# HGRN stage of a hybrid decoder step: outer products by groups of 32 partitions, read-outs in halves

## The chip, the cores and the metric

The kernel runs on one core of one Trainium2 chip. The metric is the device time of one execution in microseconds; the time before is the median of three runs.

## What is computed

The reference is one inference step of a two-layer decoder trunk for 256 prompt tokens and 8 samples of 4 tokens, width 1024. Each layer has an adaLN-modulated norm, one input projection that feeds three parallel mixers (HGRN2, RG-LRU, gated DeltaNet), an output projection, and a retrieval of experts. The change touches the HGRN2 mixer alone, and the modulation product that is woven into it:

```python
mod = jax.nn.silu(c) @ p['w_ada'] + p['b_ada']          # six sections of 1024 columns, per layer
def hgrn2_chunked(q, k, v, log_f, S0):                  # 4 heads, key and value width 64
    def step(S, inp):
        qc, kc, vc, lf = inp
        G = jnp.cumsum(lf, axis=2); Gl = G[:, :, -1]
        o_inter = jnp.einsum('bhik,bhkv->bhiv', qc * jnp.exp(G), S)
        diff = G[:, :, :, None, :] - G[:, :, None, :, :]
        decay = jnp.exp(jnp.where(mask, diff, -jnp.inf))
        A = jnp.einsum('bhik,bhjk,bhijk->bhij', qc, kc, decay)
        o = o_inter + jnp.einsum('bhij,bhjv->bhiv', A, vc)
        S = S * jnp.exp(Gl)[..., None] + jnp.einsum('bhjk,bhjv->bhkv', kc * jnp.exp(Gl[:, :, None, :] - G), vc)
        return S, o
```

The kernel does this in blocks of 8 prompt tokens in place of the reference's chunks of 64: 32 blocks for the prompt, one of 4 tokens for each sample.

## The kernel before

Everything is float32. The program is a loop over the two layers, and each layer is a row of blocks with a barrier of all engines between them: projection, local mixer, `hgrn_block`, `delta_block`, output, experts, gates, combine. Inside a block each engine runs a list that is written out by hand, and semaphores tie the lists.

`hgrn_block` has four heads in two pairs; a pair fills 128 partitions (64 rows of head r = 0 and 64 of r = 1). C = 8 is the length of a block, BLOCKS = 32, TB = 16 blocks fill one tile of 128 tokens, HALF = 8. Its parts:

- **Distances** (line 1217). For d = 0 to 7 VectorE multiplies queries by keys d tokens earlier (`pairs`, L1324), TensorE sums over a head's 64 rows with a matrix of ones (`distance(d)`, 128x128), and VectorE multiplies by the values and adds (`values`, L1341 and L1344).
- **Outer products** (`products(step)`, L1262, four steps). A token tile `ktt` (128 tokens on partitions, 64 key columns of a head) is multiplied by `vm`: the values copied 8 times side by side, each copy masked to the 8 tokens of one block (`mask_v`, ScalarE, L1183; 8 copies for each of four steps, and 8 for the samples). One matmul is 128 rows by 64 columns with 512 moving columns, and gives the outer products of 8 blocks for one head. A step has four of them (two pairs, two heads) and fills two of the four PSUM banks of `ps_outer`. `sample_products` (L1272) does the same for the samples from 32 partitions.
- **The chain of states** (L1367). VectorE forms state b = decay times state b-1 + outer product b, 64 instructions of 128x64 for the 32 blocks and two pairs. Each counts up `after0` or `after1`.
- **Read-outs** (L1233). `read_states(turn)`: for each of 8 blocks and each head TensorE multiplies the 64x64 state by 8 columns of queries, 32 small matmuls; `read_samples` does it for the states of the samples, 4 columns each.
- **Modulation tiles** (`ada(first, end)`, L532). Tiles 8 to 31 of the modulation product, each four matmuls of 128x32 with 256 moving columns. Even tiles come from `ring` (3 slots), odd ones from `extra_ring` (4 slots); the SyncE queue loads a slot again when its tile is done. After each eight tiles ScalarE copies the rows out (L556), TensorE turns them (`turn(n)`, L542), ScalarE copies the columns (L563), and the next tile after that waits for `cols_out`.

The order of TensorE decides the order of the rest. The four vm-turns use two buffers, and `mask_v` of the third turn waits for the products of the first. At the end VectorE waits for `inter_ready`, which the last read-out counts up, and adds the read-outs to the output (L1379).

`keep_busy(pe, m, out, n)` issues n bf16 matmuls of 512 columns that nobody reads. It is called in other blocks before the change.

In the rows below a float32 matmul stands as two records: the four matmuls of a products step are x8, and the 32 of a read-out are x64.

Of the kernel before, what the change touches and what calls it, by code (L numbers as in the profile page):

```python
# [27 lines left out]
P = 128  # L28
# [9 lines left out]
HD = 64  # L38
# [172 lines left out]
@contextmanager  # L211
def signals(nc, m, names):

    ctx = ExitStack()
    m.stage += 1
    sems = {n: ctx.enter_context(nc.semaphore(f"{n}_of_{m.stage}")) for n in names.split()}
    clear_retired(nc, m)
    yield sems
    m.retired.append((ctx, sems))
# [332 lines left out]
def copy_rows(act, m, s, rows, ps, n):  # L552

    e = (KD * n + KD - 1) // 2
    act.wait_ge(m.xdone[e % XRING], e // XRING + 1)
    act.activation(rows, ps[:, 0:2 * P], ACT.Copy).then_inc(s["rows_out"], 1)  # L556


def copy_columns(act, m, s, ps, n, done):

    act.wait_ge(s["cols_ready"], done)
    dst, src = ada_columns(m, SECTIONS[n], ps)
    act.activation(dst, src, ACT.Copy).then_inc(s["cols_out"], 1)  # L563
# [403 lines left out]
def keep_busy(pe, m, out, n):  # L967

    operand = m.keep[:, 0:2 * P].bitcast(BF16)
    for _ in range(n):  # L970
        pe.matmul(out, operand[:, 0:P], operand, start=True, stop=True)
# [145 lines left out]
def hgrn_block(nc, m, l, extra, stream, ps_mod):  # L1117
# [5 lines left out]
    names = ("step sums_ready turned kt_out values_done vm_ready u_ready after0 after1 samples_u sample_free sample_read "  # L1123
             "kept0 kept1 inter_ready products_ready rows_out cols_ready cols_out")
    HALF = TB // 2
    with signals(nc, m, names) as s, nc.psum_tensor("ps_sums", [P, 3, 512], F32) as ps_sums, \
            nc.psum_tensor("ps_outer", [P, 4, 512], F32) as ps_outer, nc.Block() as block:
        gate, key, since, qt, kt = m.hgate, m.hkey, m.since, m.qt, m.kt
        q = m.zact[:, 0:2, :]
        f = Area(m.big, m.after_local)  # L1130
        after = f.take(A_PAIRS, BLOCKS, HD)
        vm = f.take(2, 4, TB // 2, HD)
        pair_p = f.take(2, 2 * NP)
        pair_s = f.take(2, 2 * NB * NS)
        prod_p = f.take(2 * NP)
# [29 lines left out]
        @block.scalar  # L1165
        def _(act):
            for tt in range(3):
                n = TOK[tt][1]
                act.wait_ge(s["turned"], tt + 1)
                act.activation(flat(ktt[0:n, tt, :, :]), ps_outer[0:n, tt, 0:2 * P], ACT.Copy)  # L1170
                act.activation(vtok[0:n, tt, :], ps_outer[0:n, tt, 2 * P:4 * P], ACT.Copy).then_inc(s["kt_out"], 1)

            def mask_v(turn):

                if turn < 4:
                    tt, first, n, mask = turn // 2, turn % 2 * TB // 2, P, m.mix("block_rows")
                else:
                    tt, first, n, mask = 2, 0, NB * NS, m.mix("batch_rows")
                if turn >= 2:
                    act.wait_ge(s["u_ready"], 2 * turn - 2)  # L1180
                values = vtok[0:n, tt, :].rearrange("p (h v) -> p h v", h=4)
                for b in range(TB // 2):
                    i = act.activation(vm[0:n, turn % 2, :, b, :], values, ACT.Copy, scale=mask[0:n, first + b:first + b + 1])  # L1183
                i.then_inc(s["vm_ready"], 1)

            act.wait_ge(s["kt_out"], 3)
            mask_v(0)
            copy_rows(act, m, s, ada_rows, ps_mod, 1)
            copy_columns(act, m, s, ps_mod, 1, 1)
            mask_v(1)  # L1190
            mask_v(2)
            mask_v(3)
            copy_rows(act, m, s, ada_rows, ps_mod, 2)
            copy_columns(act, m, s, ps_mod, 2, 2)
            mask_v(4)
            copy_rows(act, m, s, ada_rows, ps_mod, 3)
            copy_columns(act, m, s, ps_mod, 3, 3)
            for pair in range(A_PAIRS):
                act.wait_ge(s[f"after{pair}"], BLOCKS)
            act.activation(m.states[:, 0:A_PAIRS, 0, :], after[:, :, BLOCKS - 1, :], ACT.Copy)  # L1200

        @block.gpsimd
        def _(pool):
# [6 lines left out]
        def _(pe):  # L1210
# [9 lines left out]
            def ada(first, end):  # L1220
                for i in range(first, end):
                    if i % KD == 0 and i > LOCAL_ADA:
                        pe.wait_ge(s["cols_out"], (i - LOCAL_ADA) // KD)
                    ada_tile(pe, m, extra, i, ps_mod)
# [7 lines left out]
                rows = slice(r * HD, (r + 1) * HD)  # L1232
                return pe.matmul(out[rows], state[rows], qt[rows, pair, t:t + n], start=True, stop=True)  # L1233

            def read_samples():

                pe.wait_ge(s["sample_free"], 1)
                for b in range(NB):
                    for pair in range(A_PAIRS):
                        for r in range(2):  # L1240
                            mm = inter(sample_inter(pair)[:, NS * b:NS * (b + 1)], pair, r, NP + NS * b, NS,
                                       m.state0[:, pair, b, :])
                mm.then_inc(s["sample_read"], 1)

            def read_states(turn):

                for pair in range(A_PAIRS):
                    pe.wait_ge(s[f"after{pair}"], HALF * (turn + 1))
                for b in range(turn * HALF + 1, min((turn + 1) * HALF + 1, BLOCKS)):
                    for pair in range(A_PAIRS):  # L1250
                        for r in range(2):
                            mm = inter(ps_sums[:, pair, C * b:C * (b + 1)], pair, r, C * b, C, after[:, pair, b - 1, :])
                return mm

            def products(step):
                pe.wait_ge(s["vm_ready"], step + 1)
                for pair in range(A_PAIRS):
                    if step >= 2:
                        pe.wait_ge(s[f"after{pair}"], HALF * (step - 1))
                    for r in range(2):  # L1260
                        rows = slice(r * HD, (r + 1) * HD)
                        mm = pe.matmul(ps_outer[rows, (2 * step + pair) % 4, :], ktt[:, step // 2, pair, rows],  # L1262
                                       vm[:, step % 2, 2 * pair + r, :, :], start=True, stop=True)
                    mm.then_inc(s["u_ready"], 1)

            def sample_products():
                pe.wait_ge(s["vm_ready"], 5)
                for pair in range(A_PAIRS):
                    pe.wait_ge(s[f"after{pair}"], HALF * 3)
                    for r in range(2):  # L1270
                        rows = slice(r * HD, (r + 1) * HD)
                        mm = pe.matmul(ps_outer[rows, pair, :], ktt[0:NB * NS, 2, pair, rows],  # L1272
                                       vm[0:NB * NS, 0, 2 * pair + r, :, :], start=True, stop=True)
                    mm.then_inc(s["samples_u"], 1)

            for tt, (t0, n) in enumerate(TOK):
                for pair in range(A_PAIRS):
# [8 lines left out]
            distance(2)  # L1286
            ada(11, 12)
            distance(3)
            ada(12, 14)
            distance(4)  # L1290
            ada(14, 16)
            distance(5)
            products(0)
            distance(6)
            turn(1)
            distance(7)
            read_samples()
            ada(16, 20)
            products(1)
            ada(20, 24)  # L1300
            products(2)
            turn(2)
            pe.wait_ge(s["values_done"], 1)
            read_states(0)
            ada(24, 27)
            products(3)
            read_states(1)
            ada(27, 29)
            sample_products()
            ada(29, 32)  # L1310
            read_states(2)
            turn(3)
            mm = read_states(3)
            mm.then_inc(s["inter_ready"], 1)

        @block.vector
        def _(ve):
# [36 lines left out]
            values(C - 1)  # L1354
            steps.wait(steps.n)
            ve.sem_inc(s["values_done"], 1)
            for turn in range(4):
                ve.wait_ge(s["u_ready"], 2 * turn + 2)
                for b in range(turn * HALF, (turn + 1) * HALF):
                    for pair in range(A_PAIRS):  # L1360
                        new, j = after[:, pair, b, :], b % HALF
                        add = ps_outer[:, (2 * turn + pair) % 4, j * HD:(j + 1) * HD]
                        if b == 0:
                            i = ve.tensor_copy(new, add)
                        else:
                            ve.wait_ge(s[f"after{pair}"], b)
                            i = ve.scalar_tensor_tensor(new, after[:, pair, b - 1, :],  # L1367
                                                        since[:, pair, C * b + C - 1:C * b + C], add, ALU.mult, ALU.add)
                        i.then_inc(s[f"after{pair}"], 1)
# [1545 lines left out]
def host_layout(a):  # L2915
# [65 lines left out]
    def const(name, value):  # L2981
        v = np.asarray(value, f)
        mixc[:v.shape[0], MIXC[name][0]:MIXC[name][1]] = v
# [19 lines left out]
    const("neg_s", np.where(same, 0.0, -1e30))  # L3003
    const("eye_c", jc == ic)
    const("eye_s", js == i_s)
    const("block_rows", j // 8 == np.arange(P // 8)[None, :])
    tok = np.arange(NB * NS) // NS
    const("batch_rows", np.tile(tok, 2)[:, None] == np.arange(NB)[None, :])
    heads_of = np.zeros((P, 6, 12))
# [65 lines left out]
```

## Time and profile before

| | us |
|---|---|
| median of three runs | 2321.52 (2315.86 to 2324.93) |
| profiled execution, its time | 2320.4 |
| profiled execution, its span | 2318.2 |
| HGRN block, layer 0, in that span | 151.57 to 194.40 |
| HGRN block, layer 1, from the first distance | 1293.90 to 1337.12 |

The span is the time from the first to the last instruction in the profile; the execution's own time has 2.2 us more around it. All times in the text are in microseconds from the span's start. PE is TensorE's matmuls, PEld its weight loads, DVE VectorE, ACT ScalarE.

### The profile page before, as it was taken

How to read it: one execution, taken by the hardware profiler on the slowest of the kernel's cores; microseconds unless marked ns; L12 is line 12 of the kernel's file. 1: busy time of each engine (PE TensorE's matmuls, PEld its weight loads, DVE VectorE, ACT ScalarE, POOL GpSimd, SP SyncE). 2: the span in 40 equal slices, each digit the busy share in tenths (PEclk: the TensorE clock that was granted, in tenths of full speed). 3: DMA queues.
4: the chain of work that ended last, by engine and by line, in shares of the span. 5: the costliest groups of instructions: out<-in, count | busy, mean ns of one | idle time of the engine just before them, and what ended most of it. 6: DMA issues, size and time to landing. Idle time of an engine off the chain costs nothing. (4 is left out here: it accounts for less than half of the span.)

```text
span 2318.2 us, 58007 instructions
## 1 busy us (share of the span) xinstructions
PE 2247.4 (97%) x20562; PEld 2076.7 (90%) x20562; DVE 1495.5 (65%) x3062; ACT 1267.3 (55%) x2437; POOL 1088.8 (47%) x990
## 2 busy tenths in 40 slices
PE   7999999999999999999989999999999999999998
PEld 4967779999998899999978586899999988999997
DVE  3876339943227878788668663598322296887885
ACT  3652225576558855555556422455855596555554
POOL 0221018864446656566304010498444474665661
PEclk8999999999999999999999889999999999999999
DMA  7472135555553389899454702455555534998982
GB/s 290 155 254 94 65 132 182 180 199 185 187 189 137 109 275 312 274 310 314 163 181 160 277 5 102 155 182 181 199 189 185 189 109 139 310 312 272 308 300 100
DMA packets 123816, 455.53 MB, mean 197 GB/s; under 512 B 13745, under 2 KB 14257, under 8 KB 122545
## 3 DMA queue, kind: packets, MB, share of 16 engines
q1 hardware_dynamic: 105264, 386.80, 46.9%
q0 software_dynamic: 18432, 67.12, 10.6%
q8 instruction: 79, 1.29, 0.2%
q14 instruction: 41, 0.33, 0.0%
HBM read 449.37 MB, written 4.49 MB: 196 GB/s over the span
## 5 line engine op out<-in xcount | busy, mean ns | idle before, releaser
L446 POOL TENSOR_TENSOR parts<-ring,parts 128x512 fp32r<-128x512 f32 x358 | 463.4, 1298 | 469.5 <-ACT parts L439 455.7
L439 ACT ACTIVATE parts<-ring 128x512 fp32r<-128x512 f32 x620 | 389.3, 632 | 352.3 <-PE ps_u L493 281.2
L489 PE MATMUL ps_u<-h_parts,parts 128*128 128x256 f32 x4096 | 563.1, 280 | 0.9 <-ACT parts L439 0.6
L2739 PE MATMUL ps_y<-act_parts,parts 128*128 128x256 f32 x4096 | 563.6, 280 | 0.0
L489 PEld LDWEIGHTS ps_u<-h_parts,parts 128*128 128x128 f32 x4096 | 514.7, 188 | 3.2 <-ACT parts L439 1.9
L2739 PEld LDWEIGHTS ps_y<-act_parts,parts 128*128 128x128 f32 x4096 | 515.8, 188 | 0.8 <-ACT parts L2679 0.7
L446 DVE TENSOR_TENSOR parts<-ring,parts 128x512 fp32r<-128x512 f32 x262 | 187.1, 720 | 360.5 <-ACT parts L439 336.1
L2788 POOL TENSOR_TENSOR act_parts<-big,act_parts 128x256 fp32r<-128x256 f32 x256 | 245.0, 957 | 306.2 <-ACT act_parts L2768 306.2
L493 PE MATMUL ps_u<-h_parts,parts 128*128 128x256 f32 x2048 | 322.2, 279 | 1.2 <-DVE parts L446 0.9
L2743 PE MATMUL ps_y<-act_parts,parts 128*128 128x256 f32 x2048 | 322.5, 279 | 0.0
L493 PEld LDWEIGHTS ps_u<-h_parts,parts 128*128 128x128 f32 x2048 | 275.5, 188 | 2.0 <-DVE parts L446 1.3
L2743 PEld LDWEIGHTS ps_y<-act_parts,parts 128*128 128x128 f32 x2048 | 276.3, 188 | 0.0
L2686 DVE TENSOR_TENSOR parts<-ring,parts 128x512 fp32r<-128x512 f32 x260 | 213.4, 843 | 75.1 <-ACT parts L2679 74.4
L2686 DVE TENSOR_TENSOR parts<-more_ring,parts 128x512 fp32r<-128x512 f32 x252 | 208.7, 848 | 74.7 <-ACT parts L2679 74.7
L2768 ACT ACTIVATE act_parts<-big 128x256 fp32r (+1 forms) x256 | 107.1, 418 | 221.3 <-PE ps_y L2743 216.2
L2679 ACT ACTIVATE parts<-ring 128x512 fp32r<-128x512 f32 x260 | 162.0, 624 | 50.2 <-PE ps_y L2743 50.2
L2679 ACT ACTIVATE parts<-more_ring 128x512 fp32r<-128x512 f32 x252 | 157.4, 625 | 46.0 <-PE ps_y L2743 46.0
L2574 POOL TENSOR_TENSOR onehot<-keep,sel 128x512 f32<-128x512 f32 x128 | 132.8, 1040 | 49.1 <-PE ps_g L2546 36.1
L2546 PEld LDWEIGHTS ps_g<-onehot 128*128 128x128 f32 x1024 | 134.5, 195 | 17.0 <-issue 13.5
L2546 PE MATMUL ps_g<-onehot 128*128 128x128 f32 x1024 | 139.7, 280 | 4.8 <-ACT onehot L2587 4.1
L489 PE MATMUL ps_z<-x_parts,parts 128*128 128x288 f32 x864 | 132.9, 296 | 1.4 <-ACT parts L439 1.4
L489 PEld LDWEIGHTS ps_z<-x_parts,parts 128*128 128x128 f32 x864 | 121.0, 188 | 2.0 <-ACT parts L439 1.7
(410 smaller groups left out, 2824.5 us busy)
## 6 DMA issues: line engine op xcount, KB each, us to landing
ring<-in_stream SPq DMA_DIRECT2D x506, 512.0 KB, 3.4
more_ring<-in_stream SPq DMA_DIRECT2D x126, 512.0 KB, 3.5
extra_ring<-in_stream SPq DMA_DIRECT2D x32, 512.0 KB, 5.9
mod_ring<-in_stream SPq DMA_DIRECT2D x32, 512.0 KB, 3.3
big<-in_stream SPq DMA_DIRECT2D x16, 512.0 KB, 11.5
out_state_out<-big SPq DMA_DIRECT2D x2, 1440.0 KB, 8.1
big<-in_state SPq DMA_DIRECT2D x2, 1280.0 KB, 10.8
big<-in_mixc SPq DMA_DIRECT2D x2, 1024.0 KB, 8.3
```

Of the source, the lines that this page charges most:

```text
L439: eng.activation(m.parts[:, q % PARTS, 0, :], half_tile(m, t, half), ACT.Copy).then_inc(s["hi_ready"], 1)
L446: eng.tensor_tensor(m.parts[:, q % PARTS, 1, :], half_tile(m, t, half), m.parts[:, q % PARTS, 0, :].bitcast(F32), ALU.subtract).then_inc(m ...
L489: pe.matmul(out, hi[:, k, :], hr[:, side, kk, 0:tokens], start=(kk + side == 0), stop=False)
L493: mm = pe.matmul(out, lo[:, k, :], hr[:, 0, kk, 0:tokens], start=False, stop=(kk == KD - 1))
L2546: mm = pe.matmul(ps_g[:, q % SETS, c, :], first[:, q % SETS, c, :], second[:, q % SETS, c, :], start=True, stop=True)
L2574: pool.tensor_tensor(second[:, g % SETS, :, :], spread(m.iota, 1, GROUP), spread(tokens_of(m.second_key, i, g), 2, P), ALU.subtract).then_ ...
L2679: act.activation(m.parts[:, q % PARTS, 0, :], tile[:, half * D // 2:(half + 1) * D // 2], ACT.Copy).then_inc(s["hi_ready"], 1)
L2686: v.tensor_tensor(m.parts[:, q % PARTS, 1, :], tile[:, half * D // 2:(half + 1) * D // 2], m.parts[:, q % PARTS, 0, :].bitcast(F32), ALU.s ...
L2739: pe.matmul(ps[:, half * KD // 2 + k, :], hi[:, k, :], act_parts[:, j % AHEAD, side, :], start=False, stop=False)
L2743: mm = pe.matmul(ps[:, half * KD // 2 + k, :], lo[:, k, :], act_parts[:, j % AHEAD, 0, :], start=False, stop=False)
L2768: act.activation(act_parts[:, j % AHEAD, 0, :], column(g, j), ACT.Copy).then_inc(s["act_hi"], 1)
L2788: pool.tensor_tensor(act_parts[:, j % AHEAD, 1, :], column(g, j), act_parts[:, j % AHEAD, 0, :].bitcast(F32), ALU.subtract).then_inc(s["ac ...
```

## The change

The mask is now by groups of 32 partitions: `block_rows` is periodic, so four masked copies serve all four groups of a token tile, and both token tiles get their copies at once (8 copies in place of 32; the samples have a buffer of their own). An outer-product matmul has 32 rows (the tokens of 4 blocks), 64 columns and 256 moving columns; the four row groups write to the four banks. There are three calls with 16, 8 and 8 matmuls in place of four with 4. `sample_products` is issued pair by pair in two places. The read-outs come in halves (4 blocks each, the samples' too) and stand between short runs of modulation tiles; the first half of the samples' stands between distances 3 and 4. `turn(3)` goes behind the last read-out, with four matmuls of `keep_busy` after it.

```diff
-            def mask_v(turn):
-                if turn < 4:
-                    tt, first, n, mask = turn // 2, turn % 2 * TB // 2, P, m.mix("block_rows")
-                else:
-                    tt, first, n, mask = 2, 0, NB * NS, m.mix("batch_rows")
-                if turn >= 2:
-                    act.wait_ge(s["u_ready"], 2 * turn - 2)
-                for b in range(TB // 2):
-                    i = act.activation(vm[0:n, turn % 2, :, b, :], values, ACT.Copy, scale=mask[0:n, first + b:first + b + 1])
+            def mask_v(tt):
+                for j in range(GROUP):
+                    i = act.activation(vm[:, tt, :, j, :], values, ACT.Copy, scale=m.mix("block_rows")[:, j:j + 1])
+            def mask_samples():
+                for b in range(NB):
+                    i = act.activation(vms[0:n, :, b, :], values, ACT.Copy, scale=m.mix("batch_rows")[0:n, b:b + 1])
             act.wait_ge(s["kt_out"], 3)
             mask_v(0)
+            mask_v(1)
             copy_rows(act, m, s, ada_rows, ps_mod, 1)
             copy_columns(act, m, s, ps_mod, 1, 1)
-            mask_v(1)
-            mask_v(2)
-            mask_v(3)
+            mask_samples()
...
-            def read_states(turn):
+            def read_states(turn, half):
+                first = turn * HALF + half * GROUP + 1
                 for pair in range(A_PAIRS):
-                    pe.wait_ge(s[f"after{pair}"], HALF * (turn + 1))
-                for b in range(turn * HALF + 1, min((turn + 1) * HALF + 1, BLOCKS)):
+                    pe.wait_ge(s[f"after{pair}"], first + GROUP - 1)
+                for b in range(first, min(first + GROUP, BLOCKS)):
...
-            def products(step):
-                pe.wait_ge(s["vm_ready"], step + 1)
+            def products(tt, first, end):
+                pe.wait_ge(s["vm_ready"], tt + 1)
                 for pair in range(A_PAIRS):
-                    if step >= 2:
-                        pe.wait_ge(s[f"after{pair}"], HALF * (step - 1))
-                    for r in range(2):
-                        rows = slice(r * HD, (r + 1) * HD)
-                        mm = pe.matmul(ps_outer[rows, (2 * step + pair) % 4, :], ktt[:, step // 2, pair, rows],
-                                       vm[:, step % 2, 2 * pair + r, :, :], start=True, stop=True)
-                    mm.then_inc(s["u_ready"], 1)
+                    if tt:
+                        pe.wait_ge(s[f"after{pair}"], GROUP * end)
+                for pair in range(A_PAIRS):
+                    for group in range(first, end):
+                        tokens = slice(32 * group, 32 * group + 32)
+                        for r in range(2):
+                            rows = slice(r * HD, (r + 1) * HD)
+                            mm = pe.matmul(ps_outer[rows, group, pair * GROUP * HD:(pair + 1) * GROUP * HD],
+                                           ktt[tokens, tt, pair, rows], vm[tokens, tt, 2 * pair + r, :, :], start=True, stop=True)
+                mm.then_inc(s["u_ready"], 1)
+            def sample_products(pair):
+                pe.wait_ge(s["vm_ready"], 3)
+                for other in range(A_PAIRS):
+                    pe.wait_ge(s[f"after{other}"], TB + GROUP * (pair + 1))
...
             distance(3)
-            ada(12, 14)
+            pe.wait_ge(s["sample_free"], 1)
+            read_samples(0, NB // 2)
             distance(4)
+            ada(12, 13)
+            distance(5)
+            products(0, 0, 4)
+            distance(6)
+            ada(13, 14)
+            distance(7)
             ada(14, 16)
-            distance(5)
-            products(0)
-            distance(6)
+            read_samples(NB // 2, NB).then_inc(s["sample_read"], 1)
             turn(1)
-            distance(7)
-            read_samples()
-            ada(16, 20)
-            products(1)
-            ada(20, 24)
-            products(2)
+            ada(16, 17)
+            pe.wait_ge(s["values_done"], 1)
+            read_states(0, 0)
+            ada(17, 19)
+            products(1, 0, 2)
+            read_states(0, 1)
+            ada(19, 21)
+            read_states(1, 0)
+            ada(21, 22)
+            products(1, 2, 4)
+            ada(22, 24)
+            read_states(1, 1)
             turn(2)
-            pe.wait_ge(s["values_done"], 1)
-            read_states(0)
+            sample_products(0)
             ada(24, 27)
-            products(3)
-            read_states(1)
+            read_states(2, 0)
             ada(27, 29)
-            sample_products()
-            ada(29, 32)
-            read_states(2)
+            read_states(2, 1)
+            ada(29, 30)
+            sample_products(1)
+            ada(30, 32)
+            read_states(3, 0)
+            read_states(3, 1).then_inc(s["inter_ready"], 1)
             turn(3)
-            mm = read_states(3)
-            mm.then_inc(s["inter_ready"], 1)
+            keep_busy(pe, m, ps_outer[:, 3, :], 4)
...
-            for turn in range(4):
-                ve.wait_ge(s["u_ready"], 2 * turn + 2)
-                for b in range(turn * HALF, (turn + 1) * HALF):
+            for first, ready in ((0, 1), (TB, 2), (TB + HALF, 3)):
+                ve.wait_ge(s["u_ready"], ready)
+                for b in range(first, TB if ready == 1 else first + HALF):
...
-    const("block_rows", j // 8 == np.arange(P // 8)[None, :])
+    const("block_rows", j // 8 % 4 == np.arange(P // 8)[None, :] % 4)
```

On ScalarE the copy of the last state now stands ahead of the third `copy_rows`, in place of behind it.

## Rows read from the trace of the kernel before

**Rows 1.** The page: busy time, share and instructions of each engine.

```profile
PE 2247.4 (97%) x20562; PEld 2076.7 (90%) x20562; DVE 1495.5 (65%) x3062; ACT 1267.3 (55%) x2437; POOL 1088.8 (47%) x990
```

**Rows 2.** Windows: HGRN block of layer 0, then the delta block's start in both layers.

```profile
core 0: us, PE busy (x) PEld busy (x) DVE busy (x) ACT busy (x) POOL busy (x), PEclk, DMA share, GB/s
151.57:194.40 42.83, 39.81 (x592) 23.64 (x593) 27.26 (x103) 19.71 (x54) 2.50 (x2) 1.00 0.76 282
194.40:203.06 8.66, 8.64 (x128) 5.84 (x128) 5.20 (x12) 2.31 (x3) 0.00 (x0) 0.61 0.01 2
...
1337.12:1344.52 7.40, 7.38 (x128) 5.19 (x128) 5.20 (x12) 2.32 (x3) 0.00 (x0) 0.72 0.01 2
```

**Rows 3.** Timeline, TensorE, layer 0 (start, length, engine, line, what, records).

```profile
139.69 5.13 PE L971 MATMUL ps_q<-keep 128*128 128x512 bf16 x23
...
168.57 0.64 PE L532 MATMUL ps_mod<-ring,cond 128*32 128x256 f32 x8
...
170.43 1.94 PE L1262 MATMUL ps_outer<-big 128*64 128x512 f32 x8
...
172.30 0.64 PE L532 MATMUL ps_mod<-ring,cond 128*32 128x256 f32 x8
...
174.17 1.94 PE L1262 MATMUL ps_outer<-big 128*64 128x512 f32 x8
...
176.59 0.64 PE L542 MATMUL ps_mod<-keep,big 128*128 128x36 f32 x4 [0.48 <-ACT big L556]
...
188.68 2.04 PE L1233 MATMUL ps_sums<-big 64*64 64x8 f32 x64
190.65 0.64 PE L542 MATMUL ps_mod<-keep,big 128*128 128x36 f32 x4
191.21 1.80 PE L1233 MATMUL ps_sums<-big 64*64 64x8 f32 x56
194.42 0.99 PE L1486 MATMUL ps_delta<-big 128*128 128x6 f32 x4 [1.41 <-PEq L1127]
```

**Rows 4.** Timeline, VectorE, layer 0.

```profile
167.12 0.28 DVE L1344 TENSOR_TENSOR big<-big 128x64 f32<-128x64 f32 x1
...
172.42 3.16 DVE L1367 SCALAR_TENSOR_TENSOR big<-big,ps_outer 128x64 f32<-128x64 f32 x16 [1.84 <-PE ps_outer L1262]
...
193.06 0.67 DVE L1379 TENSOR_TENSOR big<-big,ps_sums 128x496 f32<-128x496 f32 x1 [4.94 <-PE ps_sums L1233]
```

**Rows 5.** Windows, TensorE alone: two stretches of 64x64 matmuls in the delta block.

```profile
core 0: us, PE busy (x), PEclk, DMA share, GB/s
201.36:202.95 1.59, 1.59 (x97) 1.00 0.03 10
206.08:207.63 1.55, 1.55 (x51) 1.00 0.04 11
```

**Rows 6.** Timeline, ScalarE, layer 0: masked copies, and columns after a turn.

```profile
154.01 3.31 ACT L1183 ACTIVATE big<-big 128x256 f32<-128x256 f32 x8
...
177.26 0.24 ACT L563 ACTIVATE mod<-ps_mod 128x72 f32<-128x72 f32 x1 [0.72 <-PE ps_mod L542]
```

**Rows 7.** DMA issues from 160 to 194 (KB each, median us to landing).

```profile
ring<-in_stream SPq DMA_DIRECT2D x10, 512.0 KB, 3.5
```

**Rows 8.** Windows around falls of the granted clock (columns as in rows 2).

```profile
190.97:194.39 3.42, 2.04 (x59) 1.91 (x59) 0.67 (x1) 0.44 (x3) 0.00 (x0) 1.00 0.05 16
194.39:197.80 3.41, 3.38 (x18) 2.57 (x18) 2.95 (x7) 1.27 (x1) 0.00 (x0) 0.50 0.00 0
...
1310.54:1313.96 3.42, 3.42 (x24) 1.18 (x18) 1.14 (x6) 3.42 (x10) 0.00 (x0) 0.50 0.73 247
```

**Rows 9.** Timeline, TensorE, layer 1.

```profile
1309.67 0.64 PE L532 MATMUL ps_mod<-ring,cond 128*32 128x256 f32 x8
...
1315.04 0.64 PE L532 MATMUL ps_mod<-ring,cond 128*32 128x256 f32 x8
...
1333.40 2.34 PE L1233 MATMUL ps_sums<-big 64*64 64x8 f32 x56
```

More of the change, by code:

```diff
@@ L1125, in hgrn_block @@
     HALF = TB // 2
+    GROUP = 32 // C
     with signals(nc, m, names) as s, nc.psum_tensor("ps_sums", [P, 3, 512], F32) as ps_sums, \
@@ L1131, in hgrn_block @@
         after = f.take(A_PAIRS, BLOCKS, HD)
-        vm = f.take(2, 4, TB // 2, HD)
+        vm = f.take(2, 4, GROUP, HD)
+        vms = f.take(4, NB, HD)
         pair_p = f.take(2, 2 * NP)
@@ L1171, in _ @@
                 act.activation(vtok[0:n, tt, :], ps_outer[0:n, tt, 2 * P:4 * P], ACT.Copy).then_inc(s["kt_out"], 1)
-            def mask_v(turn):
-                if turn < 4:
-                    tt, first, n, mask = turn // 2, turn % 2 * TB // 2, P, m.mix("block_rows")
-                else:
-                    tt, first, n, mask = 2, 0, NB * NS, m.mix("batch_rows")
-                if turn >= 2:
-                    act.wait_ge(s["u_ready"], 2 * turn - 2)
-                values = vtok[0:n, tt, :].rearrange("p (h v) -> p h v", h=4)
-                for b in range(TB // 2):
-                    i = act.activation(vm[0:n, turn % 2, :, b, :], values, ACT.Copy, scale=mask[0:n, first + b:first + b + 1])
+            def mask_v(tt):
+                values = vtok[:, tt, :].rearrange("p (h v) -> p h v", h=4)
+                for j in range(GROUP):
+                    i = act.activation(vm[:, tt, :, j, :], values, ACT.Copy, scale=m.mix("block_rows")[:, j:j + 1])
+                i.then_inc(s["vm_ready"], 1)
+            def mask_samples():
+                n = NB * NS
+                values = vtok[0:n, 2, :].rearrange("p (h v) -> p h v", h=4)
+                for b in range(NB):
+                    i = act.activation(vms[0:n, :, b, :], values, ACT.Copy, scale=m.mix("batch_rows")[0:n, b:b + 1])
                 i.then_inc(s["vm_ready"], 1)
@@ L1187, in _ @@
             mask_v(0)
+            mask_v(1)
             copy_rows(act, m, s, ada_rows, ps_mod, 1)
             copy_columns(act, m, s, ps_mod, 1, 1)
-            mask_v(1)
-            mask_v(2)
-            mask_v(3)
+            mask_samples()
             copy_rows(act, m, s, ada_rows, ps_mod, 2)
             copy_columns(act, m, s, ps_mod, 2, 2)
-            mask_v(4)
-            copy_rows(act, m, s, ada_rows, ps_mod, 3)
-            copy_columns(act, m, s, ps_mod, 3, 3)
             for pair in range(A_PAIRS):
@@ L1200, in _ @@
             act.activation(m.states[:, 0:A_PAIRS, 0, :], after[:, :, BLOCKS - 1, :], ACT.Copy)
+            copy_rows(act, m, s, ada_rows, ps_mod, 3)
+            copy_columns(act, m, s, ps_mod, 3, 3)
         @block.gpsimd
@@ L1233, in inter, with read_samples @@
                 return pe.matmul(out[rows], state[rows], qt[rows, pair, t:t + n], start=True, stop=True)
-            def read_samples():
-                pe.wait_ge(s["sample_free"], 1)
-                for b in range(NB):
+            def read_samples(first, end):
+                for b in range(first, end):
                     for pair in range(A_PAIRS):
@@ L1242, in read_samples @@
                                        m.state0[:, pair, b, :])
-                mm.then_inc(s["sample_read"], 1)
-            def read_states(turn):
+                return mm
+            def read_states(turn, half):
+                first = turn * HALF + half * GROUP + 1
                 for pair in range(A_PAIRS):
-                    pe.wait_ge(s[f"after{pair}"], HALF * (turn + 1))
-                for b in range(turn * HALF + 1, min((turn + 1) * HALF + 1, BLOCKS)):
+                    pe.wait_ge(s[f"after{pair}"], first + GROUP - 1)
+                for b in range(first, min(first + GROUP, BLOCKS)):
                     for pair in range(A_PAIRS):
@@ L1266, in sample_products @@
-            def sample_products():
-                pe.wait_ge(s["vm_ready"], 5)
-                for pair in range(A_PAIRS):
[L1269 to L1274, printed above, removed]
+                    if tt:
+                        pe.wait_ge(s[f"after{pair}"], GROUP * end)
@@ new lines, in products @@
+                mm.then_inc(s["u_ready"], 1)
[3 more added lines that the diff above has]
+                    pe.wait_ge(s[f"after{other}"], TB + GROUP * (pair + 1))
+                for r in range(2):
+                    rows = slice(r * HD, (r + 1) * HD)
+                    mm = pe.matmul(ps_outer[rows, pair, :], ktt[0:NB * NS, 2, pair, rows],
+                                   vms[0:NB * NS, 2 * pair + r, :, :], start=True, stop=True)
+                mm.then_inc(s["samples_u"], 1)
@@ L1356, in _ @@
             ve.sem_inc(s["values_done"], 1)
-            for turn in range(4):
-                ve.wait_ge(s["u_ready"], 2 * turn + 2)
-                for b in range(turn * HALF, (turn + 1) * HALF):
+            for first, ready in ((0, 1), (TB, 2), (TB + HALF, 3)):
+                ve.wait_ge(s["u_ready"], ready)
+                for b in range(first, TB if ready == 1 else first + HALF):
                     for pair in range(A_PAIRS):
-                        new, j = after[:, pair, b, :], b % HALF
-                        add = ps_outer[:, (2 * turn + pair) % 4, j * HD:(j + 1) * HD]
+                        new = after[:, pair, b, :]
+                        add = ps_outer[:, b // GROUP % 4, (pair * GROUP + b % GROUP) * HD:(pair * GROUP + b % GROUP + 1) * HD]
                         if b == 0:
```

## The prediction

> **What bounds the kernel now.** I read the page first: TensorE is busy 97% of the span, VectorE 65%, ScalarE 55% [rows 1]. The reader is to see that only what shortens TensorE's list, or lets it run at full clock, can shorten the kernel. Then the window of the block that is changed, in layer 0: of its 42.83 us TensorE is busy 39.81, VectorE 27.26 and ScalarE 19.71 [rows 2]. Then the timeline of TensorE, in which I take the time of a piece from its start to the next piece's start, since the lengths overlap [rows 3]. Last VectorE's timeline: it waits 1.84 us for outer products in one place and 4.94 us for the last read-outs [rows 4], so the block ends by TensorE's list, then one VectorE instruction (193.06 to 193.73), then the barrier: TensorE starts the next block at 194.42, 0.69 later.
>
> **Pieces of TensorE's list** [rows 3]. Four modulation tiles: 168.57 to 170.43, 1.86. An outer-product step: 170.43 to 172.30, 1.87. A read-out of 8 blocks: 188.68 to 190.65, 1.97. A turn: 190.65 to 191.21, 0.56. Each contains a fixed part. A bf16 matmul of 512 columns takes 0.216 (23 of them 5.13, the last one 0.38 of it), one cycle of 2.4 GHz a column. A step's eight float32 records of 512 columns, the two heads' side by side, take 1.87 / 4 = 0.47 a pair of records, so two cycles a column, 0.427, and a rest: 4 x 0.427 = 1.71 and 0.16, which goes into the change of piece; for four modulation tiles it is 1.86 - 4 x 0.427 = 0.15. I take 0.15 for every change between shapes of tiles.
>
> **Outer products.** Before, four steps stream 4 x 1.71 = 6.83 a layer. After, 32 matmuls of 256 columns do it. One tile of 32 rows by 64 columns then has, in each of the three calls, two matmuls of two records of 256 columns: 4 x 0.213 = 0.85. If the tiles run side by side the three calls stream 3 x 0.85 = 2.56, which saves 4.27. If matmuls that share columns and differ in rows run one after the other, the 32 are 16 head pairs of 0.427, 6.83 again, and nothing is saved. The trace has no 32-row tiles of this kind, but it has 64-row ones: in the first stretch of [rows 5] all four 64x64 tiles are in use, and 97 records take 1.59 us, 16 ns each; in the second only the two diagonal ones, and 51 take 1.55 us, 30 ns each. Same matmul, twice the rate when the rows differ too. With eight tiles a record of the new call is due each 0.85/32 = 27 ns, slower than the 16 ns already reached, so issue is no bound. I take the full 4.27; the bounds are 0 and 4.27.
>
> The Trainium skill says as much (TensorE: Matmul & The Clock Gate, Part 3, packing small matmuls), and gives 3.07x for four row tiles; by that factor the first call would stream 0.85 x 4 / 3.07 = 1.11, 0.26 us a layer more, an estimate from that page. No row here shows that factor. The Trainium skill also speaks against the change (TensorEngine Tiling, Key Properties): a change of tiling mode drains the engine. By the trace that is within the 0.15 us above.
>
> **More changes of piece.** From distance 0 to the end I count 29 pieces before and 40 after: 5 more runs of modulation tiles, 4 more read-outs, 2 more of 128x128 (distance 6, the turn and distance 7 were one). 11 x 0.15 = 1.65; the read-outs' fixed part is rather 0.11 (1.97 less 64 records at 29 ns), so 1.5. The bounds are 0 (if the loads ahead hide them) and 2.2 (11 x 0.20, what a full 128-column load would add).
>
> **Waits.** Before, step 3 ends at about 174.17 + 1.87 = 176.04 and turn(2) starts at 176.59, 0.55 late, since it waits for the copy of rows; after, a read-out lies between, and this goes. But turn(1) now stands right ahead of tile 16, which waits for ScalarE's columns: the copy starts 0.67 after the turn and takes 0.24 [rows 3, 6], so tile 16 starts 0.99 after turn(1) where 0.56 would do: +0.43. Turn(3) goes behind the last read-out, so VectorE's last addition comes 0.56 sooner.
>
> Sum to VectorE's last addition: -4.27 + 1.5 - 0.55 + 0.43 - 0.56 = **-3.45**: it starts at about 189.6 and ends at 190.3.
>
> **What else must keep up.** The VectorE chain: 16 instructions in 3.16 [rows 4], so 0.395 a block, 12.6 for 32. In my list of starts the last distance is at 165.3, its values end near 166.4 (167.40 before), and half the chain ends at 172.8. The second call needs blocks 0 to 7 (169.7) and runs at 171.3 to 172.3; the third runs at 176.0 to 177.0, where VectorE waits about 1.1; the chain ends at 180.3, and the last read-outs, which need it, are due at 187.7. It has 7 us to spare. The masked copies: 8 take 3.31 [rows 6]; 24 fewer spare ScalarE 9.9 us that nobody waited for, and both sets are there at 157.3, six us before use. The loads: the ring slot of tile 24 is free at 181.1 and its next load, tile 30, is used at 186.9, against 3.5 from issue to landing [rows 7]; other tiles have more. With a wait there it would cost up to 1 us.
>
> **The end of the block.** Behind the last read-out (189.4) come turn(3), 0.56, and four busy matmuls. At 0.216 each these are 0.86: TensorE ends at about 190.9, 0.6 behind VectorE. If the barrier takes the same 0.69, the next block starts at 191.6, **2.8 sooner** than 194.42. The two layers have the same list: **-5.6**.
>
> **The clock.** In 190.97 to 194.39 TensorE streams almost nothing (read-outs of 8 columns, then 1.41 idle), and from 194.39 it has half clock, 1.2 GHz [rows 3, 8]. The delta block's first pieces take 8.66 in layer 0 at a mean clock of 0.61, that is 6.8 us at the half level, and 7.40 at 0.72, 4.1 us, in layer 1 [rows 2]. So each us at the half level costs (8.66 - 7.40) / (6.8 - 4.1) = 0.47 us: 3.2 in layer 0, 1.9 in layer 1. Layer 1's last read-out is longer too, 2.34 for 1.80 [rows 3, 9]: 0.5. A further fall is in the middle of layer 1's block, 1310.54 to 1313.96 [rows 8], behind the uncut read-out of the samples; tiles 16 to 19 and one outer step take 5.37 there (1309.67 to 1315.04) and 3.73 in layer 0 (168.57 to 172.30) [rows 3, 9]: 1.6. Together 7.3 us. The change cuts the read-outs in two between denser pieces, and the end has 0.86 us of full columns and some 0.7 idle in place of 1.41. Yet read-outs and a turn still fill 2.3 us there, so I count on two thirds of the 7.3: **-4.9**. The bounds are 0 and -7.3, plus up to 2 more falls elsewhere, of 1.6 each.
>
> Sum: 2320.4 - 5.6 - 4.9 = 2309.9 for the profiled execution. The median of the runs is 1.1 above it, so I predict **2311**.
>
> **Rivals.**
> - The order helps and the clock doesn't: it falls at the ends as before. For it: the sparse 2.3 us. Then 2321.5 - 5.6 = 2316 (2313 to 2319). Chance 0.25.
> - All clock is kept, in the delta block too, which has sparse stretches that depend on where it starts: 2321.5 - 5.6 - 7.3 - 2 = 2306 or less. Chance 0.12.
> - Slower: row groups don't run side by side. Then 4.27 a layer isn't saved, and from -2.8 becomes +1.5: +3.0 in two layers, 2324.5 with no clock regained. It decides from the point at which the three calls save less than 2.8 a layer. Against it speak [rows 5]. Chance 0.05.
> - VectorE becomes the bound. If the third call came so late that the chain's last 3.16 us stood ahead of the last read-outs, each us over the 7 of slack would be lost. Its price would be all of the gain, 2319 to 2322; chance 0.04. The Trainium skill (TensorEngine Tiling, PSUM Bottleneck) says that tiling speeds TensorE and not the emptying of its banks; by [rows 4] the slack is there.
> - New falls of the clock in the middle, two of 1.6 a layer, and none regained: 2321.5 - 5.6 + 6.4 = 2322. Chance 0.04.
>
> The forecast's own case, 2307 to 2315, has 0.50.
>
> **How the numbers follow.** 0.5% of 2321.5 is 11.6 us, about what a measurement of this kernel can tell from no change (the three runs lie 9 us apart). Faster than that is below 2309.9: the 0.12 of the case with all clock kept and about half of the forecast's 0.50, in all 0.36. Slower than that, above 2333, needs the slower rival and more: 0.02. The rest, 0.62, is within. The range 2304 to 2320 leaves out the best part of the second case and the slow ones.
>
> **What would show it.** L1262 as 32 rows by 64 columns: 32 records in about 1.1 us for the first call, against 8 in 1.94; were it 3.4, the row groups were serial. VectorE's last addition at about 189.6 in layer 0. The next block 2.8 sooner. Granted clock 1.00 in the stretch after it. If the clock there is 0.5 in both layers, the time is 2316; if the block is shortened by less than 2, the changes of piece cost more than 0.15 each.

## The result, and the profile after

The changed kernel takes 2339.96 us (median of 9 runs, 2330.20 to 2343.52) against 2319.05 (9 runs): ratio 1.0084, 95% interval 1.0072 to 1.0095. It is **slower** by 21 us, 0.8%, where 2311 was forecast and 2304 to 2320 was the range. The profiled execution has a span of 2338.1.

Windows of the changed kernel: layer 0's block from the first distance, split at 171.2, and layer 1's from the fall of the clock on (columns as in [rows 2]):

```profile
155.67:171.20 15.53, 15.20 (x214) 9.14 (x214) 13.12 (x50) 4.83 (x14) 0.00 (x0) 1.00 0.76 246
171.22:215.60 44.38, 44.08 (x439) 25.49 (x437) 14.94 (x61) 5.28 (x13) 0.00 (x0) 0.50 0.47 158
...
1321.51:1365.90 44.39, 44.09 (x442) 25.52 (x439) 15.02 (x61) 5.38 (x13) 0.00 (x0) 0.50 0.49 164
```

The reader is to see the granted clock: 1.00 for 15.5 us, then 0.50 for 44.4, and the same again in layer 1. Before, the whole block of layer 0 ran at 1.00 [rows 2].

Timeline, TensorE, of the changed kernel, layer 0:

```profile
164.74 1.12 PE L1268 MATMUL ps_outer<-big 32*64 32x256 f32 x32
...
168.14 1.10 PE L1235 MATMUL ps_sums<-big 64*64 64x4 f32 x32
169.17 0.64 PE L542 MATMUL ps_mod<-keep,big 128*128 128x36 f32 x4
170.13 0.64 PE L532 MATMUL ps_mod<-ring,cond 128*32 128x256 f32 x8 [0.33 <-ACT mod L563]
170.70 1.48 PE L1235 MATMUL ps_sums<-big 64*64 64x8 f32 x32
172.11 1.08 PE L532 MATMUL ps_mod<-extra_ring,cond 128*32 128x256 f32 x8
172.97 1.08 PE L532 MATMUL ps_mod<-ring,cond 128*32 128x256 f32 x8
173.98 1.98 PE L1268 MATMUL ps_outer<-big 32*64 32x256 f32 x16
...
210.01 0.99 PE L1504 MATMUL ps_delta<-big 128*128 128x6 f32 x4 [0.30 <-PEq L1128]
```

The first call of outer products, 32 records of 32 rows by 64 columns, takes 1.12 us. It does the work of two of the four steps of before, 1.94 each [rows 3]. Up to here everything is as worked out. Then come, one behind the other, a read-out, a turn, a wait of 0.33 for the columns, one tile and a read-out. From 171.2 on, at half clock, each piece takes nearly twice its time, and none of the runs of modulation tiles that follow is longer than three.

### The profile page after: what moved, and what is told of

The parts are those of the page before. It is cut to its first block and busy times, and to the rows that moved or that the text cites. A ratio compares the mean times of both kernels' runs of the same rounds, so it can differ in the third digit from the quotient of the medians.

```text
span 2338.1 us, 58111 instructions
## 1 busy us (share of the span) xinstructions
PE 2269.9 (97%) x20634; PEld 2087.2 (89%) x20634; DVE 1496.9 (64%) x3062; ACT 1248.2 (53%) x2389; POOL 1092.3 (47%) x990
```

## The experiments

Theories A and B are stated in the first expectation, C and D in the fifth. The kernel before was timed again with each group of runs, and each ratio is to those times. Each run has one profiled execution.

`fill(n)` issues n bf16 matmuls of 192 columns that nobody reads ("busy matmuls"), 80 to 90 ns each, and some 0.1 us more for the change of piece. Where it is used, VectorE adds the samples' read-outs behind `inter_ready` (not in the third run).

**1. The order alone.**

```diff
-products(0, 0, 4); products(1, 0, 2); products(1, 2, 4)
+products(0); products(1) ... products(2) ... products(3)      # 128 rows, 512 columns, in these places
```

> The new order of TensorE's list and the halved read-outs, but the outer products by 128 rows as before (a third buffer for the masked values, so that no step waits for a buffer). Theory A (the order holds the clock down: short runs of modulation tiles between read-outs never make a dense stretch, so the clock doesn't come back after its fall at turn(1)): half clock for 20 us or more in each layer's block, some 2340 to 2350 us. Theory B (the row-group products do it, because they take 4.3 us of full columns out of a layer): the clock stays, only the pieces cost, 2318 to 2324 us.

2326.44 us (2308.01 to 2336.69), ratio 1.0026 (1.0001 to 1.0051). Both theories are off: the order costs a third of the loss, and the executions lie far apart. Of its 7 us the prediction's sum gives 3 to the pieces (the -5.6 without the 8.5 that the row groups save). In its profile the clock falls at 174.7 and is back after 3.4 us, in which TensorE did a tile and one outer-product step of 128 rows (175.54, 3.22 us); it falls again at 188.4 and stays at half for 23.9 us. Layer 1 shows the same: 3.3 us from 1318.2, with a step, and 23.9 from 1331.7.

**2. The row groups alone.**

```diff
-products(0) ... ada(16, 20); products(1); ada(20, 24); products(2) ... products(3)
+products(0, 0, 4) ... ada(16, 24); products(1, 0, 2) ... products(1, 2, 4)     # the rest in the old order
```

> The products by 32 rows in the order of before: whole read-outs, tiles 16 to 23 in one run, turn(3) ahead of the last read-out, no busy matmuls. Theory A: the clock falls as it did before, at the ends and perhaps once in the middle, so the 4.3 us a layer stay as a gain: 2308 to 2314 us. Theory B: half clock through the block, above 2330 us.

2335.23 us (2319.33 to 2340.02), 1.0054 (1.0028 to 1.0080). Theory A, that the order does it, has fallen, since the old order loses as well. The time is what theory B expected, but this run's timeline, TensorE, shows a possible cause that neither theory had:

```profile
171.99 0.61 PE L532 MATMUL ps_mod<-extra_ring,cond 128*32 128x256 f32 x8
174.99 1.08 PE L532 MATMUL ps_mod<-ring,cond 128*32 128x256 f32 x8 [2.39 <-DMA ring<-in_stream]
```

With no outer products between them, tiles 16 to 23 come faster than the loads. TensorE idles 2.39 us, and has half clock from 175.0 to 216.0. In layer 1 it idles 2.80 us at the same place and the clock falls too, but it comes back for 3 us in the middle of the later call on two row groups, behind three tiles:

```profile
1335.19 1.25 PE L1268 MATMUL ps_outer<-big 32*64 32x256 f32 x16
```

Such a call takes 1.98 at half clock and 1.09 at full. The changed kernel has no such wait.

**3. Busy matmuls round turn(1).**

```diff
 read_samples(NB // 2, NB).then_inc(s["sample_read"], 1)
+fill(12)
 turn(1)
+fill(6)
```

> The changed kernel with 12 bf16 matmuls of 192 columns ahead of turn(1) and 6 behind it, some 1.4 us of added work in a layer, part of it in the 0.4 us wait for the columns. If the fall at turn(1) is what starts the 44 us of half clock and the rest of the order holds a full clock, the time drops to 2305 to 2318 us. If the order behind it loses the clock by itself, the fall only moves to a later place and the time stays at 2330 to 2345 us.

2320.62 us (2306.62 to 2328.14), 0.9997 (0.9976 to 1.0018): a little above what was expected, and 19 us less than the changed kernel, for 1 us a layer of work more. The clock now holds to 188.4, and falls there, in the stretch of the samples' products and halved read-outs, for 17 us. In layer 1 it holds to 1335.3, the last turn, and is at half for 10 us. The run also gives the changed order's starts at full clock (its timeline, TensorE):

```profile
155.54 1.29 PE L1219 MATMUL ps_sums<-big 128*128 128x512 f32 x4 [1.12 <-DVE big L1349]
...
178.29 1.09 PE L1268 MATMUL ps_outer<-big 32*64 32x256 f32 x16
```

The third call starts 22.75 behind the first distance. The prediction had it at 176.0, 21.77 behind its 154.23; the busy matmuls ahead of the turn add 1.0 (169.04 to 170.04).

**4. The tail alone**, in the kernel before.

```diff
-turn(3); read_states(3)
+read_states(3); turn(3); keep_busy(pe, m, ps_outer[:, 3, :], 4)
```

> The kernel before with only its tail changed: turn(3) behind the last read-out and four busy matmuls. VectorE's last addition 0.56 earlier, TensorE's end about 0.3 to 0.8 later. If the busy matmuls hold the clock at the block's end: 3 to 5 us less, 2314 to 2317 us. If not: 2318 to 2322 us.

2318.52 us, 0.9989 (0.9974 to 1.0003): nothing that can be told from none. In its profile the clock is at half from 195.1 to 205.3: the busy matmuls (196.41) come when it has already fallen, behind two whole read-outs in a row. An earlier fall, at 181.4, ended after 3.3 us, in a 128-row step (182.47, 3.10 us).

**5. Busy matmuls where the row groups took work out**, in the second run's kernel.

```diff
 products(0, 0, 4)
+fill(11)
-ada(16, 24)
+ada(16, 20); fill(21); ada(20, 24)
 products(1, 0, 2)        # and the same behind products(1, 2, 4)
+fill(11)
```

> The second run's kernel (products by 32 rows in the old order, 2335 us) with 54 busy bf16 matmuls of 192 columns a layer, some 4.3 us, in the places from which the row groups took the streaming of 128 rows; the samples' addition stands behind the last read-out, 0.5 us later. Theory C (what counts is how much of the time all 128 rows are fed; the row groups took 4.3 us of that out, so the clock falls and doesn't return): the clock is that of the kernel before, 0.98 to 0.99, and the time 2316 to 2324 us, less than without the added work. Theory D (the 32-row shape itself keeps the clock down): the clock stays at 0.973 to 0.981 and the time is 2340 us or more.

2317.48 us (2312.41 to 2323.71), 0.9999 (0.9987 to 1.0012): theory C. 4.7 us a layer of work that nobody reads (the four fills of its timeline, each to the next piece's start) gives back 18 us. It doesn't show by which way, since the busy matmuls also slow the tiles, and the wait for the load shrinks from 2.39 to 0.60 us.

**6. The second token tile in one call**, in the changed kernel.

```diff
-ada(17, 19); products(1, 0, 2); read_states(0, 1); ada(19, 21); read_states(1, 0); ada(21, 22); products(1, 2, 4); ada(22, 24)
+ada(17, 19); read_states(0, 1); ada(19, 21); products(1, 0, 4); read_states(1, 0); ada(21, 24)
```

> The changed kernel with the second token tile's products in one call of 16 matmuls over all four row groups, in place of two calls that use two row groups each. 0.85 us of streaming and one change of piece less a layer. Theory C: the call feeds 128 rows for 0.85 us where two calls fed 64 for 1.7, the sum is the same, and the read-outs round it are as sparse: the clock falls at turn(1) as in the changed kernel, 2330 to 2342 us. If the half-filled calls are what keeps the clock down: 2315 to 2325 us.

2317.56 us (2305.50 to 2324.93), 0.9994 (0.9975 to 1.0013). Theory C as I had put it, a sum of work, missed this: the first fall is where it was, but the clock comes back. Two windows of this run, of layer 0:

```profile
171.60:178.40 6.80, 6.80 (x94) 3.90 (x100) 2.45 (x13) 1.63 (x5) 0.00 (x0) 0.50 0.88 331
178.40:188.70 10.30, 9.87 (x214) 6.16 (x200) 7.02 (x35) 0.93 (x3) 0.00 (x0) 1.00 0.87 295
```

And its timeline, TensorE, where they meet, and at the same call and the return of the clock in layer 1:

```profile
177.29 1.63 PE L1268 MATMUL ps_outer<-big 32*64 32x256 f32 x32
178.85 1.10 PE L1235 MATMUL ps_sums<-big 64*64 64x8 f32 x32
...
1317.91 2.01 PE L1268 MATMUL ps_outer<-big 32*64 32x256 f32 x32
...
1324.38 1.50 PE L1235 MATMUL ps_sums<-big 64*64 64x8 f32 x32
```

In layer 0 the clock comes back in the middle of the one call that feeds all four row groups. The changed kernel's calls feed two groups, 64 of 128 rows, for the same sum, and the clock stayed down through both. But in layer 1 the clock falls at 1311.8, the joined call passes wholly at half clock, and full clock is back only at 1325.2, behind three tiles in a row, which this edit makes too (`ada(21, 24)` in place of one and two). So the run shows that the clock can come back in this order; it doesn't show that the joined call is what brings it back. In layer 0 it falls again at 188.7, for 17 us.

**7. Busy matmuls throughout**, in the changed kernel: `fill` of 2 to 12 at twelve places between its pieces (74 a layer; the 72 of the expectation is a miscount) and two more in `keep_busy` at the end. The samples' second read-out goes behind turn(1); all shapes are kept.

```diff
-read_samples(NB // 2, NB).then_inc(s["sample_read"], 1)
+fill(6)
 turn(1)
+fill(2)
+read_samples(NB // 2, NB).then_inc(s["sample_read"], 1)
 ada(16, 17)
+fill(4)
...
-keep_busy(pe, m, ps_outer[:, 3, :], 4)
+keep_busy(pe, m, ps_outer[:, 3, :], 6)
```

> The changed kernel with busy matmuls of 192 columns at twelve places, 72 a layer and two more at the end, some 8 us of added work a layer with the changes of piece. Theory C: no sparse stretch is left, the clock stays full in both blocks (0.99), and the time is 2319.5 - 5.6 - 7.3 + 17 = 2324 us or a little less: 16 us of work added and 16 us less time than the changed kernel. Otherwise 2345 us or more.

2318.81 us (2314.51 to 2322.56), 1.0002 (0.9991 to 1.0012). Some 7 us of work more a layer by its timeline, and 21 us less time than the changed kernel. Windows of this run, over both layers' blocks:

```profile
153.00:199.00 46.00, 45.06 (x707) 28.98 (x708) 26.32 (x105) 10.14 (x26) 0.45 (x1) 1.00 0.73 248
1296.00:1342.00 46.00, 45.64 (x795) 29.92 (x788) 26.70 (x105) 7.84 (x19) 0.00 (x0) 1.00 0.67 227
```

The granted clock is 1.00 in both. So the 32-row shape doesn't keep it down, nor does the order if its gaps are filled.

**8 to 10, 12. An order made for the clock**: one call for the second tile; the samples' second read-out behind turn(1), in the wait for the columns; sparse pieces apart. The whole list from tile 14 on:

```python
 ada(14, 16); fill(5); turn(1); read_samples(NB // 2, NB); ada(16, 19); read_states(0, 0); ada(19, 21); read_states(0, 1)
 products(1, 0, 4); ada(21, 22); read_states(1, 0); ada(22, 24); sample_products(0); turn(2); fill(5); ada(24, 26)
 read_states(1, 1); ada(26, 27); sample_products(1); ada(27, 29); read_states(2, 0); ada(29, 31); fill(4)
 read_states(2, 1); fill(10); read_states(3, 0); ada(31, 32); fill(6); read_states(3, 1); turn(3); keep_busy(..., 4)
 # 9: also fill(4) behind ada(21, 22), fill(5) ahead of ada(26, 27) and of ada(27, 29)
 # 10: none of the fills;  12: as 9, and fill(6) ahead of and behind ada(19, 21)
```

> An order made from theory C: the second tile's products in one call, no two sparse pieces side by side where a run of tiles can stand between them, and 30 busy matmuls of 192 columns a layer round the turns and the last read-outs. Work a layer at full clock: the changed kernel's 2.8 us gain, less 2.9 for the busy matmuls, their changes of piece and the samples' addition at the end, plus 1.0 for the single call. Theory C: the clock holds in most executions, 2308 to 2316 us. If it falls at turn(1) all the same: 2325 us or more.

> The even order with 14 more busy matmuls of 192 columns a layer (44 in all), at three places in the stretch in which the second layer's clock fell at 1316.1 in the even order's profile. Some 1.7 us a layer of work more with the changes of piece, partly in a wait for a load. Theory C: the fall goes, all executions lie at a clock of 0.988 or more, 2308 to 2314 us. If this has no effect on the clock: 2319 to 2322 us.

> The even order without any of the 30 busy matmuls (the four at the end stay): what the order alone does. Theory C: stretches with two sparse pieces come back round the turns and the last read-outs, the clock falls in more executions, 0.980 to 0.985, and the 2.9 us a layer of work that is saved is lost again: 2314 to 2322 us. If the order alone holds the clock: 2306 to 2311 us.

> The even order with 44 busy matmuls and 12 more a layer round tiles 19 and 20, where the first layer's clock fell at 173.6 in that run's profile; 0.96 us and some 0.4 for the changes of piece a layer. Theory C: that fall goes as well; all executions at 0.988 or more, 2309 to 2314 us, and none above 2320. If the few slow executions of the run before have another cause, they stay.

| busy matmuls a layer | median (range), us | ratio, 95% interval |
|---|---|---|
| 0 (run 10) | 2318.16 (2311.56 to 2333.36) | 1.0001 (0.9989 to 1.0012) |
| 30 (run 8) | 2317.73 (2304.61 to 2324.50) | 0.9987 (0.9966 to 1.0008) |
| 44 (run 9) | 2312.27 (2305.51 to 2331.51) | 0.9984 (0.9965 to 1.0004) |
| 56 (run 12) | 2312.98 (2307.91 to 2318.31) | **0.9977 (0.9965 to 0.9989)** |

Each step adds work, and none adds time that can be told from noise. Run 8 was above its range of 2308 to 2316. Run 9's median was in its range, but not all its executions. Run 12 has none above 2320, though two have a mean clock of 0.987, below the 0.988 expected; its profile's clock is 1.00 in layer 0's block up to 193.9 and in layer 1's up to 1330.5. It is the only version shown faster than both kernels, by 5 us of the kernel before and 27 of the changed one. It is the best of four tries, and runs 9 and 12 can't be told apart. Run 10 differs from the other three in VectorE's list too, which is that of the changed kernel.

Run 10's profiled execution, its slowest (2333.36), speaks against the joined call as the thing that ends a fall. Two windows of it:

```profile
172.80:210.20 37.40, 36.77 (x356) 20.90 (x348) 12.53 (x46) 3.24 (x7) 0.00 (x0) 0.50 0.44 157
1319.80:1357.20 37.40, 36.77 (x384) 21.82 (x382) 11.87 (x45) 2.71 (x6) 0.00 (x0) 0.50 0.44 159
```

The joined call stands right at the start of the first (172.62), and the clock stays at half for 37.4 us in each layer.

**11. One call, and turn(1) covered.**

```diff
-ada(14, 16); read_samples(NB // 2, NB); turn(1)      # in run 6's kernel
+ada(14, 16); fill(5); turn(1); read_samples(NB // 2, NB)
```

> The changed kernel with two changes: the second tile's products in one call, and five busy matmuls ahead of turn(1) with the samples' second read-out behind it, in the wait for the columns. The first alone gave 2317.6 us. Theory C: the fall at turn(1), 7 to 14 us of half clock a layer in that run's profile, goes: 2309 to 2315 us. Otherwise 2316 us or more.

2315.71 us (2311.39 to 2327.43), 1.0006 (0.9990 to 1.0021). The median is just above the 2309 to 2315 expected, and the ratio shows no gain over run 6. The clock falls at 170.6 all the same, so covering turn(1) alone doesn't prevent the early fall.

## Why the prediction was wrong

**Right: the pieces.** The row groups run side by side: 32 records in 1.12 us, 1.05 to the next piece, 1.01 worked out (0.85 streamed, 0.16 for the change). The estimate by the factor 3.07, 1.11 of streaming, isn't borne out: 1.05 less 0.16 leaves 0.89. The wait for the columns: tile 16 starts 0.96 behind turn(1), 0.99 worked out. The third call in run 3 is within 0.1 of its worked-out place. VectorE's chain has its 0.36 + 5.83 for the first 16 blocks, and TensorE never waited for the chain. Run 7 gives the whole block at full clock: 44.23 from the first distance (153.59) to the next block (197.82), of which 7.3 are its fills and 0.4 its two more matmuls in `keep_busy`; 36.5 are left, against 40.19 - 2.8 = 37.4 worked out. So -5.6 for two layers stands as the gain of the pieces at full clock, and the rival of serial row groups is out. One reading was wrong and small: "other tiles have more" time for their loads than tile 30, yet in run 3 tile 28 waits 0.45 for its load. A check: mean clocks of 0.984 before and 0.972 after are 2 x 0.016 x 2318 = 74 and 2 x 0.028 x 2338 = 131 us at the half level. 57 us more at the prediction's 0.47 is 27 us; the span grew by 19.9, so some 7 us of gain is hidden in it.

**Wrong: the step "I count on two thirds of the 7.3: -4.9", with the bounds "0 and -7.3, plus up to 2 more falls elsewhere, of 1.6 each".** The sign was wrong: with -5.6 from the pieces and a span 19.9 longer, the clock's term was about +25, not -4.9. Each fall was priced as one of 3.4 us, because in the kernel before the fall of 1310.54 ended by 1313.96 [rows 8]. I didn't ask what TensorE did while it lasted. Timeline of the kernel before:

```profile
1310.56 1.10 PE L532 MATMUL ps_mod<-ring,cond 128*32 128x256 f32 x8
...
1312.45 2.66 PE L1262 MATMUL ps_outer<-big 128*64 128x512 f32 x8
```

There it did the last two of four tiles in a row and then an outer-product step of 128 rows, in whose course the clock came back. The change takes such stretches away. In the changed kernel the fall at 171.2 met only runs of one to three tiles, calls on half the rows and read-outs, so 44.4 us passed, to the delta block's wide matmuls. From the first distance to the next block it is 54.34 (155.67 to 210.01) against 40.19 before, 14.2 more although the pieces save 2.8: a fall priced at 1.6 cost some 17 in layer 0's block. The rival "new falls of the clock in the middle" had the right place and the wrong price, and a chance of 0.04.

**What the change did to the clock.** Shown: the time went to the clock, and the loss begins at turn(1). Run 7 keeps the shapes and, but for one read-out, the order, has full clock through both blocks, and is 21 us faster than the changed kernel with more work. In the changed kernel half a read-out, the turn, 0.33 idle, one tile and half a read-out lie in a row there; run 3, which fills that place, has its falls 17 and 21 us later behind the first distance, is at half clock for 17 and 10 us in place of 44 and 44, and gets 19 us back.

Not shown: which part of the change keeps the clock down once it has fallen. The nearest reading is that steps of 128 rows became calls on 64. For it: in runs 1 and 4, and in the kernel before, a fall in the middle ended within 3.4 us, in such a step, and run 6, which joins two calls, gets 22 us back, some 2 of them for the work that it spares. Against it: in run 2's layer 1 the clock came back in a call on 64 rows; in run 6's layer 1 and all through run 10's profile the joined call didn't bring it back. The longer run of tiles in run 6 is a rival that no run tests apart. The order alone costs 7 us (run 1). That it does so by spreading halved read-outs between short runs of tiles is argued from its timeline, not shown. Run 7 shows that neither shape nor order matters where no sparse stretch is left.

**Left open:** how much of run 2's loss is its wait for a load, and why executions of one kernel differ so much (those of run 8 lie 20 us apart, those of run 9 26, with mean clocks from 0.981 to 0.991 and 0.980 to 0.992). Only one execution of each has a profile, so where the others lose the clock isn't known, and a fall seen in one profile, or missing from it, is one draw.

## What to carry to other kernels

Where TensorE bounds the kernel, packing its matmuls so that they take less time can also take away the dense stretches that kept its clock up; here a saving of 2.8 us a layer came with a loss of some 17 in layer 0. Price a fall of the clock by what follows it, and look in the trace for what TensorE did when the falls that are there ended: it was 3.4 us in one order and 44.4 in another. When sparse pieces must be issued, try them one at a time between long runs, and try some matmuls that nobody reads: here 56 of them, 5.7 us a layer by run 12's timeline, gained 5 us by the medians over the same order without them.

## What the runs showed of the hardware

- Eight tiles of 32 rows by 64 columns run side by side: 32 records of 256 float32 columns in 1.05 us, where calls on two row groups took 1.02 us for 16 (run 3, at full clock, each to the next piece's start).
- The granted clock fell after a stretch with much small work in it even though TensorE counted as busy 2.67 of 3.00 us in it (window of the changed kernel):

```profile
168.00:171.00 3.00, 2.67 (x58) 1.99 (x56) 3.00 (x17) 1.54 (x5) 0.00 (x0) 1.00 0.96 287
```

- At half clock it stayed through stretches in which TensorE was busy nearly all the time (44.08 of 44.38 us, 171.22 to 215.60) with tiles, read-outs and calls on 64 rows, and came back behind the delta block's wide matmuls, at 215.6.
- With busy matmuls at twelve places between the same pieces it stayed at 1.00 for 46 us in both layers (run 7).

The Trainium skill (TensorE: Matmul & The Clock Gate, HAM oscillation) warns of idle gaps. Run 2 agrees, where 2.39 us idle came right before the fall; but in the changed kernel the fall came with 0.33 us idle, so a high share of busy time didn't keep the clock.
